# PEER gates: the first one-hot laid out token by token, by eight comparisons with a per-token operand

## The reference

```python
q = (h @ w_q).reshape(T, PEER_HEADS, 2, D_HALF)
s = jnp.einsum('thpe,pke->thpk', q, sub_keys)              # two scores of 128 keys each, 8 heads
s1, i1 = lax.top_k(s[:, :, 0], PEER_TOPK)
s2, i2 = lax.top_k(s[:, :, 1], PEER_TOPK)
cand = (s1[..., :, None] + s2[..., None, :]).reshape(...)
top_s, top_c = lax.top_k(cand, PEER_TOPK)
e1 = jnp.take_along_axis(i1, top_c // PEER_TOPK, axis=-1)
e2 = jnp.take_along_axis(i2, top_c % PEER_TOPK, axis=-1)
expert = e1 * N_KEYS + e2                                  # one of 128 x 128 experts
g = jax.nn.softmax(top_s, axis=-1)
a = jnp.einsum('td,thkd->thk', h, u_tab[expert])
y = jnp.einsum('thk,thkd->td', g * jax.nn.gelu(a), v_tab[expert])
```

## Time and profile before

| | |
|---|---|
| median of 3 runs | 2773.17 us (2771.75 to 2774.8) |
| profiled execution | 2774.84 us, span 2773.0 us |
| mean granted clock of TensorE | 0.958 |
| instructions | 48133 |
| DMA | 348.87 MB, mean 126 GB/s |

### The profile page before, as it was taken

How to read it: one execution, slowest core, us unless ns; L and a number is a source line. 1 busy time by engine, 2 the same in 40 slices (tenths; PEclk the granted TensorE clock), 3 DMA queues, 4 the chain that set the end, 5 groups by cost and what they waited for, 6 DMA issues and landing times.

```text
span 2773.0 us, 48133 instructions
## 1 busy us (share of the span) xinstructions
PE 2643.8 (95%) x19531; PEld 2430.2 (88%) x19531; DVE 1418.8 (51%) x2614; ACT 809.1 (29%) x1066; POOL 1287.5 (46%) x570
## 2 busy tenths in 40 slices
PE   8898998999999999999899989999999999999997
PEld 3586977999999999999877869779999999999997
DVE  1122298668743770772155122986687437707721
ACT  2312312342253244224201123123422532442242
POOL 0321401555576567556611014015555765675564
PEclk9999999999999999999997579999999999999998
DMA  4333343333344334334654013433333443343342
GB/s 178 106 126 104 125 136 122 122 106 111 118 159 145 122 132 157 124 119 139 190 171 136 0 63 135 137 121 121 107 108 120 154 150 121 126 163 122 121 137 78
DMA packets 51243, 348.87 MB, mean 126 GB/s; under 512 B 6112, under 2 KB 6128, under 8 KB 11408
## 3 DMA queue, kind: packets, MB, share of 16 engines
q1 hardware_dynamic: 44928, 324.16, 34.2%
q0 software_dynamic: 6192, 22.95, 2.9%
HBM read 342.83 MB, written 4.26 MB: 125 GB/s over the span
## 4 chain that ended last, share of the span: by engine, by line
PE 92%; DVE 4%; POOL 2%; issue 1%; ACT 1%; DMA 0%; POOLq 0%; DVEq 0%; ACTq 0%
PE ps L629 17%; PE ps L630 16%; PE ps L635 16%; PE ps L603 11%; PE ps L619 9%; PE ps L529 3%; PE ps L552 2%; PE ps L807 2%; PE ps L484 2%; PE ps L485 2%; PE ps L486 2%; POOL w_lo L392 2%; DVE C_lo L1337 1%; PE ps L741 1%; PE ps L728 1%; PE ps L511 1%
## 5 line engine op out<-in xcount | busy, mean ns | idle before, releaser
L392 POOL TENSOR_TENSOR w_lo<-ring,w_hi 128x1024 fp32r<-128x1024 f32 x448 | 1124.8, 2511 | 963.1 <-PE ps L630 677.7
L965 ACT ACTIVATE w_hi<-ring 128x1024 fp32r<-128x1024 f32 x448 | 473.6, 1058 | 780.4 <-PE ps L630 779.8
L629 PE MATMUL ps<-C_hi,w_hi 128*128 128x288 f32 x2048 | 628.9, 307 | 22.1 <-DVE C_lo L1337 17.8
L635 PE MATMUL ps<-C_hi,w_lo 128*128 128x288 f32 x2048 | 606.1, 296 | 0.0
L630 PE MATMUL ps<-C_lo,w_hi 128*128 128x288 f32 x2048 | 605.5, 296 | 0.0
L629 PE MATMUL ps<-h_hi,w_hi 128*128 128x288 f32 x1536 | 465.3, 303 | 8.9 <-POOL w_lo L392 5.4
L630 PE MATMUL ps<-h_lo,w_hi 128*128 128x288 f32 x1536 | 454.7, 296 | 0.0
L635 PE MATMUL ps<-h_hi,w_lo 128*128 128x288 f32 x1536 | 454.4, 296 | 0.0
L629 PEld LDWEIGHTS ps<-C_hi,w_hi 128*128 128x128 f32 x2048 | 393.5, 192 | 27.4 <-DVE C_lo L1337 13.5
L630 PEld LDWEIGHTS ps<-C_lo,w_hi 128*128 128x128 f32 x2048 | 390.0, 190 | 0.0
L635 PEld LDWEIGHTS ps<-C_hi,w_lo 128*128 128x128 f32 x2048 | 388.5, 190 | 0.0
(11 more groups left out here) (211 smaller groups left out, 2663.8 us busy)
## 6 DMA issues: line engine op xcount, KB each, us to landing
ring<-in_U SPq DMA_DIRECT2D x128, 1024.0 KB, 4.9
ring<-in_V SPq DMA_DIRECT2D x128, 1024.0 KB, 4.9
ring<-in_peer_q SPq DMA_DIRECT2D x16, 1024.0 KB, 4.8
ring<-in_w_in_v SPq DMA_DIRECT2D x8, 1024.0 KB, 7.0
ring<-in_w_in_u SPq DMA_DIRECT2D x8, 1024.0 KB, 4.9
ring<-in_w_out SPq DMA_DIRECT2D x8, 1024.0 KB, 4.9
work<-in_cache POOLq DMA_DIRECT2D x8, 512.0 KB, 5.5
big<-in_cache POOLq DMA_DIRECT2D x8, 512.0 KB, 7.2
```

Source lines behind the costliest of these rows:

```text
L392: pool.tensor_tensor(w_lo[:, k % LO_SLOTS, :], ring[:, k // 2, (k % 2) * HBLK:(k % 2 + 1) * HBLK], w_hi[:, k % HI_SLOTS, :], ALU.subtract) ...
L629: one = pe.matmul(out, w_hi[:, h % HI_SLOTS, at], hi, start=start, stop=False)
L635: return pe.matmul(out, w_lo[:, h % LO_SLOTS, at], hi, start=False, stop=stop)
L965: act.activation(w_hi[:, k % HI_SLOTS, :], ring[:, bl % R, (k % 2) * HBLK:(k % 2 + 1) * HBLK], ACT.Copy).then_inc(hi_made, 1)
```

## The change

`hot1` is laid out (slot of the ring, token, e1), so that the 128 columns of a token are contiguous, and TensorE's stationary operand is read accordingly. The one comparison of 1024 elements with a broadcast tensor becomes eight comparisons of 128 elements, one for each token, in each of which `iota_row` (0 to 127 in f16) is compared with an operand of one f32 value per partition. For that `halves` is split into `e1_of` (f32) and `e2_of` (f16).

```diff
@@ -172,9 +172,11 @@
         C_lo = at_address("C_lo", big_at, [P, 2, EQ, T], F32R)
         stat, _ = place("stat", [P, 16])
         warm, _ = place("warm", [P, 8])
-        halves, _ = place("halves", [P, 2, T], F16)
+        e1_of, _ = place("e1_of", [P, T])
+        e2_of, _ = place("e2_of", [P, T], F16)
         parts, _ = place("parts", [P, GATE_PARTS, T], F16)
         iota16, _ = place("iota16", [P, NK, GT], F16)
+        iota_row, _ = place("iota_row", [P, NK], F16)
         iota_top, _ = place("iota_top", [P, TOP])
         ident, _ = place("ident", [P, P])
         ident_r, _ = place("ident_r", [NSAMP, NSAMP], F32R)
@@ -234,7 +236,7 @@
         gsum = view(work, 1920, 2 * PH + SH)
         grec = view(work, 1944, 2 * PH + SH)
         eg = view(work, 1968, 3, 3, P)
-        hot1 = hots[:, 0:1024].bitcast(F16).rearrange("p (r e t) -> p r e t", r=RH, t=GT)
+        hot1 = hots[:, 0:1024].bitcast(F16).rearrange("p (r t e) -> p r t e", r=RH, t=GT)
         hot2 = hots[:, 1024:1536].bitcast(F16).rearrange("p (r c e t) -> p r c e t", r=RH, c=GATE_PARTS, t=GT)
         here2 = hots[:, 1536:1664].bitcast(F16).rearrange("p (e t) -> p e t", t=GT)
         C = view(big, 0, 2, EQ, T)
@@ -600,7 +602,7 @@
                         pe.wait_ge(gate_free, it * GR + (nth * NGG + j - 1 + CREDIT))
                         for t in range(GT):
                             for c in range(GATE_PARTS):
-                                g = pe.matmul(ps[:, 6 + j % 2, t * EQ:(t + 1) * EQ], hot1[:, j % RH, :, t],
+                                g = pe.matmul(ps[:, 6 + j % 2, t * EQ:(t + 1) * EQ], hot1[:, j % RH, t, :],
                                               hot2[:, j % RH, c, :, t], start=(c == 0), stop=(c == GATE_PARTS - 1))
                         g.then_inc(gate_full, 1)
 
@@ -1183,6 +1185,7 @@
             dve.wait_ge(consts_loaded, 16 * 3)
             dve.tensor_copy(iota_top[:], iota[:, 0:TOP])
             dve.tensor_copy(iota16[:], iota.unsqueeze(2).broadcast_to((P, NK, GT)))
+            dve.tensor_copy(iota_row[:], iota)
             for k in range(NX):
                 dve.wait_ge(x_loaded[k], 16)
             norm("na", 1, 0, split=0)
@@ -1296,7 +1299,8 @@
                     dve.tensor_copy(slots[:, :, t0:t0 + tn],
                                     ps[:, b, 0:3 * tn].rearrange("p (a b) -> p a b", a=3)).then_inc(dve_free, 1)
                 dve.wait_ge(dve_free, D0[f"e{layer}"] + 3)
-                dve.tensor_copy(halves[:], slots[:, 0:2, :])
+                dve.tensor_copy(e1_of[:], slots[:, 0, :])
+                dve.tensor_copy(e2_of[:], slots[:, 1, :])
                 for c in range(GATE_PARTS):
                     link(dve.tensor_copy(parts[:, c, :], slots[:, 2, :]))
                     if c + 1 < GATE_PARTS:
@@ -1311,9 +1315,10 @@
                     if before:
                         dve.wait_ge(hot_ready, before)
                     step(dve.tensor_tensor(here2, iota16[:, q * EQ:(q + 1) * EQ, :],
-                                           halves[:, 1, tok].unsqueeze(1).broadcast_to((P, EQ, GT)), ALU.is_equal))
-                    dve.tensor_tensor(hot1[:, s], iota16[:],
-                                      halves[:, 0, tok].unsqueeze(1).broadcast_to((P, NK, GT)), ALU.is_equal)
+                                           e2_of[:, tok].unsqueeze(1).broadcast_to((P, EQ, GT)), ALU.is_equal))
+                    for t in range(GT):
+                        dve.tensor_scalar(hot1[:, s, t, :], iota_row[:], e1_of[:, j * GT + t:j * GT + t + 1], None,
+                                          ALU.is_equal)
                     last_step()
                     dve.tensor_tensor(hot2[:, s], here2.unsqueeze(1).broadcast_to((P, GATE_PARTS, EQ, GT)),
                                       parts[:, :, tok].unsqueeze(2).broadcast_to((P, GATE_PARTS, EQ, GT)),
```

## The result

The changed kernel takes 2800.65 us (median of 4 runs, 2796.99 to 2802.86) against 2772.46 for the kernel before, measured beside it (4 runs). The ratio is 1.010, 95% interval 1.0082 to 1.0117: slower, as forecast, but by 28 us and not by 81. The profiled execution has a span of 2797.5 us, 24.5 more than before.

What follows compares the result with a forecast made beforehand. TensorE bounds the kernel, with VectorE, held behind GpSimd's subtraction, near its limit in gate stretches. Losses of 48 (wide rounds), 30 (packed rounds) and 3 us make 81 on 2773: 2854 us, range 2772 to 2950.

Steps and rivals of the forecast that it cites:

- 0.163 us start to start: VectorE, one new comparison: 0.067 fixed, 0.06 for the per-partition operand, 0.033 for 128 elements; 0.71 us more per group.
- The 3 us for the two groups ahead of C_lo: Start of the packed stretch: two groups built before C_lo pieces TensorE waits for add 2 x 0.71 us per layer.
- the order of TensorE's waits: Sign: TensorE idle 50 to 90 us before gate matmuls, per group most in the packed stretch, least in the first.
- 4 us for a round of the three wide stretches: Loss per round of 18 gate groups using 15 of 16 halves; bounds 0 and 7.9; 12 rounds give 48 us.
- 7.5 for one of the packed stretch: Loss per round in down(0, 1), groups packed into 12 of 16 halves; 4 rounds give 30 us.
- 78.0 if nothing of VectorE's lies beside GpSimd: Wide round after the change: GpSimd's 38.6 us plus 18 x 2.19 of VectorE on one path, against TensorE's 70.1.
- the 5.9 us over: Wide round: path's excess over TensorE's 70.1 us, being 7.9 less some 2 for L1327 beside L392.
- the two groups of lead: VectorE enters a round with two groups built ahead and uses that lead up before TensorE waits; 4 us taken.
- about half: Packed rounds: about half of VectorE's idle time (6.6 and 11.1 us) should vanish when it runs late.
- rival 1: TensorE's weight loads get shorter, saving a group about 0.4 us if VectorE keeps up: faster, 2737 us, chance 0.10.
- GpSimd's mean: Sign: mean time of GpSimd's subtraction L392 should fall from 2.51 us to near 2.45.
- Rivals 2 and 3: Rival 2: comparisons cost 0.10 us, 2777 us, chance 0.10. Rival 3: lower pace, 2932 or about 3075 us, chance 0.20.

Runs made afterwards that it cites:

- run 5: Changed kernel with a constant in place of the per-partition operand in each of the eight comparisons: 2759.8 us, ratio 0.995 to the kernel before.
- run 2: Changed kernel with eight comparisons into the contiguous layout, but TensorE reading the columns 8 elements apart as before: 2815.7 us, ratio 1.015 to the kernel before.
- run 11: Changed kernel with the moving operand also read from contiguous addresses (columns mixed up): 2822.6 us, ratio 1.0185 to the kernel before.

## Why the prediction went wrong in its size

**Right.** The mechanism and the sign. One comparison was to cost 0.163 us start to start and eight 1.31, against 0.60: measured 0.163 and 1.31, and 0.81 without the operand. The Trainium skill's figure ("VectorE: DVE Perf Modes", section on the TRN2 errata; an estimate of 0.094 us) comes near the median of 0.102 measured with a constant (run 5), and misses the 0.163 with an operand per partition. The comparisons are held, too. In the first stretch eight that begin at 470.86 take 3.54 us, with an L394 inside:

```profile
470.86 3.54 DVE L1320 TENSOR_SCALAR hots<-iota_row,e_of 128x128 f16<-128x128 f16 x8
```

```profile
471.07 2.46 POOL L394 TENSOR_TENSOR w_lo<-ring,w_hi 128x1024 fp32r<-128x1024 f32 x1 [9.33 <-PE ps L632]
```

The 3 us for the two groups ahead of C_lo are right as well: the way into the packed stretch grew by 1.2 us in the first layer and 1.3 in the second. So is the order of TensorE's waits, most per group in the packed stretch.

**Wrong, the main term: what a round loses.** I took 4 us for a round of the three wide stretches and 7.5 for one of the packed stretch. With VectorE's part alone (run 2) they lost 1.8 to 2.1 and 4.0 (half of the table's differences). The step that failed is the price of an L392 on the path: "78.0 if nothing of VectorE's lies beside GpSimd", less 2 us for one L1327 in three or four, charges VectorE 2.41 us per L392 in the packed stretch and some 2.28 in the others. I took that from a VectorE that still had idle time. A VectorE that is always busy meets GpSimd otherwise: GpSimd's instruction has to wait for it first, and in the packed stretch it mostly gets in where L1332 starts, so that L1332 or L1349 lies beside the subtraction. I counted the hold in the timelines of the first layer, as time of VectorE's instructions above their undisturbed durations, and the idle time as what is missing to the stretch's length:

| | up(1) | down(0), packed | down(1) |
|---|---|---|---|
| VectorE idle, us per stretch: before, in run 2 | 53.8, 1.7 | 21.3, 12.0 | 34.1, 1.4 |
| hold, us per subtraction: before, in run 2 | 0.91, 2.07 | 1.83, 1.63 | 1.51, 2.01 |

In the wide stretches the idle time vanished, as I had it, but a subtraction cost 2.0 to 2.1 us and not 2.28. Over the 15 or 16 of a round that is an estimated 3 to 4 us, which turns the 5.9 us over into the 2 or so that were measured, without the two groups of lead that I had also counted on. In the packed stretch (27 subtractions, a few of them in its middle, where no group is built) "about half" of the idle time was right: 9.3 of 21.3 us vanished. What failed there is the fixed hold, which fell from 49.3 to 44.1 us over the stretch.

Over the whole run the same count gives 96 + 120 + 142 = 358 us before (L1313, L1315, L1318 at 0.28, 0.68 and 0.41), and 357 + 125 + 0 = 482 after (L1317 at 0.28, eight L1320 at 1.38, L1323 at 0.41). Two of the lines before, beside L1315 in the earlier trace rows:

```profile
L1318 DVE TENSOR_TENSOR hots<-hots,parts 128x512 f16<-128x512 f16 x288 | 260.2, 904 | 0.0
...
L1313 DVE TENSOR_TENSOR hots<-iota,halves 128x256 f16<-128x256 f16 x288 | 176.8, 614 | 0.3
```

The eight comparisons add 201 us of their own and the hold grows by 124. Against these stand VectorE's waits for TensorE, before and after:

```profile
DVE big L1327 <- PE ps L603: 462.6, 104, 70.7
...
DVE xT L1344 <- PE ps L635: 309.2, 58, 12.9
```

```profile
DVE big L1332 <- PE ps L605: 266.6, 15, 64.6
DVE xT L1349 <- PE ps L637: 229.2, 26, 12.3
...
PE ps L605 <- DVE hots L1323: 33.2, 60, 0.7
```

The two waits fell by 276 us, so idle time took up 276 of the 310 us by which VectorE is busier.

**Wrong, the smaller term: TensorE's group.** "[...] nothing in this trace says that their 1.05 us depend on it, so 0" was no more than the lack of a row. (The 1.05 us are a duration, too; start to start it is 1.02.) Contiguous stationary columns are worth 0.09 us per group, 24 us alone and 15 on top of VectorE's part. This is rival 1 in kind but not in size, for the group can't go below 0.93 while the moving operand sits 16 bytes apart, and it doesn't rescue a kernel whose pace VectorE sets. The rule of the Trainium skill that I set beside it ("SBUF — State Buffer", note on cache lines) agrees in direction. The note also says that two hits in a line of 16 bytes are enough for full bandwidth. The runs show no such step but a gradual gain: 0.97 us at 8 bytes, which is two columns in a line, 0.94 at 4, 0.93 contiguous.

In sum: VectorE 43 instead of 81, TensorE -15 instead of 0, which is the 28 measured. Both errors made the forecast too high. That the time still falls into the stated range says little for the sum, for the range began at the time before. Of the signs, GpSimd's mean did not fall (2513 ns, 2511 before), for it still has to wait, as the L394 of 2.69 us above shows, and TensorE's wait of 33.2 us is below the 50 to 90 forecast. Rivals 2 and 3 were refuted as to their mechanism, the price of a comparison. Rival 2's price came true with a constant operand, and there the time was 2760, not 2777, since TensorE's gain was in it.

## What to carry to other kernels

Before one large instruction is replaced by eight small ones, count the fixed costs: 0.102 us for a comparison of 128 elements here, of which an estimated 0.067 are fixed, and 0.06 more for a per-partition operand. And first look for a layout in which the large one keeps its fast form (pairs were enough). What a hold costs is no constant: one and the same subtraction cost VectorE 0.9 us in the mean where VectorE had idle time, 2.0 where it had none, and 1.6 in the packed stretch. The sum that charged it at nearly its whole 2.41 us came out almost twice too high. And when an operand of a matmul is laid out anew, look at both: here one alone gave at most 24 us, and both 142.

## What the runs showed of the hardware that I had not expected

A load of 128 f16 columns and a matmul of 32 take 64 ns with both operands 16 bytes apart, 63 with only the stationary one so, 58 with only the moving one so, and 26 with neither (the group's 1.02, 1.00, 0.93 and 0.42 us by 16). This is where 132 us of this kernel lay, in a place where the stationary operand alone showed 24 us and the moving one alone nothing. And making TensorE faster made the changed kernel 22 us slower (run 11). VectorE was held at other places, and TensorE's longer pauses went together with falls of its clock; the runs don't say how much either costs.
